# Scan mixer: in-chunk products copied out by ScalarE and added by GpSimd, VectorE's recurrence in one piece

## The reference, cut to what matters

```python
def s5_mixer(h, lam_re, ..., d_skip, w_glu):
    u = hf.reshape(b, s, S5_GROUPS, S5_GROUP)
    y_fwd = _s5_direction(u, ..., False)     # hs[t] = lam_bar * hs[t-1] + B u[t];  y = Re(C hs)
    y_bwd = _s5_direction(u, ..., True)
    y = (y_fwd + y_bwd).reshape(b, s, d) + d_skip.astype(jnp.float32) * hf
    g = jax.nn.gelu(y).astype(h.dtype)
    val, gate = jnp.split(g @ w_glu, 2, axis=-1)
    return val * jax.nn.sigmoid(gate)
```

## Time and profile before

| | us |
|---|---|
| median of 3 runs (lowest, highest) | 3253.74 (3252.61, 3254.21) |
| the profiled execution's own time | 3251.42 |
| its span, first to last instruction | 3249.6 |
| PE busy | 2966.4 (91%) |
| DVE, ACT, POOL busy | 1560.2, 1078.3, 248.3 |

### The profile page before, as it was taken

The page is one execution under the profiler, slowest core; times in us unless marked ns, Lnnn a source line. Parts: engine busy times, 40 slices in busy tenths (PEclk is TensorE's granted clock), DMA queues, the critical chain, the costliest instruction groups (busy, mean ns, idle before and its releaser), DMA issues.

```text
span 3249.6 us, 39097 instructions
## 1 busy us (share of the span) xinstructions
PE 2966.4 (91%) x15982; PEld 2394.7 (74%) x15982; DVE 1560.2 (48%) x2276; ACT 1078.3 (33%) x1651; POOL 248.3 (8%) x230
## 2 busy tenths in 40 slices
PE   6999997489999989989999699998999998898977
PEld 5787887377888877777787478887888886665745
DVE  5775663934434434534434654344544344534444
ACT  4332332143212224525435232222332233422233
POOL 2332220200000000000000300000100000100000
PEclk9999998699999989989999899999999999987868
DMA  3254547243443221122121322222122222111000
GB/s 111 87 160 153 154 140 244 102 141 110 123 130 104 91 91 59 52 85 74 70 95 68 128 80 103 91 104 78 58 98 92 103 91 87 53 40 39 14 26 27
DMA packets 109956, 305.30 MB, mean 94 GB/s; under 512 B 27616, under 2 KB 67872, under 8 KB 80464
## 3 DMA queue, kind: packets, MB, share of 16 engines
q1 hardware_dynamic: 104656, 281.31, 26.3%
q10 hardware_dynamic: 5120, 21.50, 1.8%
HBM read 265.11 MB, written 41.85 MB: 94 GB/s over the span
## 4 chain that ended last, share of the span: by engine, by line
PE 80%; DVE 8%; ACT 3%; issue 2%; POOL 2%; DMA 1%; SPq 0%; DVEq 0%; ACTq 0%; POOLq 0%
PE ps L94 79%; DVE s_ L121 2%; PE ps L99 1%; DVE H_ L121 1%; DVE htf_ L135 1%; ACT htf_ L117 0%; ACT hh_ L117 0%; ACT wh_ L117 0%; DVE ol_ L121 0%; DVE Pm_ L121 0%; DVE nmx_ L143 0%; ACT R_ L117 0%; DVE R_ L121 0%; DVE R_ L135 0%; ACT PT_ L117 0%
## 5 line engine op out<-in xcount | busy, mean ns | idle before, releaser
L94 PE MATMUL ps<-hh_,wh_ 128*128 128x512 f32 x2184 | 869.5, 398 | 22.2 <-DVE hl_ L121 11.1
L94 PE MATMUL ps<-hl_,wh_ 128*128 128x512 f32 x2184 | 854.8, 391 | 0.0
L94 PE MATMUL ps<-hh_,wl_ 128*128 128x512 f32 x2184 | 854.4, 391 | 0.0
L121 DVE TENSOR_TENSOR wl_<-raw_,wh_ 128x2048 fp32r<-128x2048 f32 x209 | 480.9, 2301 | 550.4 <-ACT wh_ L117 550.4
L117 ACT ACTIVATE wh_<-raw_ 128x2048 fp32r<-128x2048 f32 x209 | 399.0, 1909 | 358.0 <-PE ps L94 339.7
L94 PEld LDWEIGHTS ps<-hh_,wh_ 128*128 128x128 f32 x2184 | 412.9, 189 | 122.0 <-DVE hl_ L121 9.2
L94 PEld LDWEIGHTS ps<-hl_,wh_ 128*128 128x128 f32 x2184 | 413.4, 189 | 87.2 <-issue 3.7
L94 PEld LDWEIGHTS ps<-hh_,wl_ 128*128 128x128 f32 x2184 | 412.9, 189 | 87.5
L94 PE MATMUL ps<-ah_,wl_ 128*128 128x512 f32 x704 | 279.5, 397 | 0.0
L94 PE MATMUL ps<-ah_,wh_ 128*128 128x512 f32 x704 | 278.3, 395 | 0.0
L94 PE MATMUL ps<-al_,wh_ 128*128 128x512 f32 x704 | 277.7, 395 | 0.0
(11 more groups left out here) (319 smaller groups left out, 3734.7 us busy)
## 6 DMA issues: line engine op xcount, KB each, us to landing
raw_<-in_w SPq DMA_DIRECT2D x209, 1024.0 KB, 4.9
sO<-s5ce_ SPq DMA_DIRECT2D x32, 256.0 KB, 4.0
sW<-s5wt_ SPq DMA_DIRECT2D x16, 512.0 KB, 3.7
sA<-os_ SPq DMA_DIRECT2D x24, 256.0 KB, 2.1
ol_<-sA SPq DMA_DIRECT2D x24, 256.0 KB, 3.6
sT<-sK SPq DMA_DIRECT2D x32, 128.0 KB, 3.4
sB<-mk_ SPq DMA_DIRECT2D x8, 510.0 KB, 7.7
wh_<-sW ACTq DMA_DIRECT2D x3, 1024.0 KB, 4.8
```

The source lines that it names most:

```text
L94: return self.e.matmul(out, lhsT, rhs, start=start, stop=stop, skip_group_check=True)
L121: return Nothing() if self.e is None else self.e.tensor_tensor(out, a, b, op)
```

## The change

Three things change. ScalarE copies each result of `same` from PSUM to SBUF (into the yb buffers, which are free then), between its table loads. GpSimd adds that copy to U right after its multiplication, in place of VectorE. VectorE runs the recurrence of both halves to the end without any addition between (`LEAD` goes from 18 to 24); the bias additions (`mk_<-ps,mk_`, for the next layer) and the additions of `outputs` come after it.

```diff
-LEAD = 18
+LEAD = 24
@@ s5_scalar
-    for i in range(12, NT):
+    for i in range(12, 16):
         table_load(K, ac, i)
+    for un in range(4):
+        for h in range(2):
+            k = 2 * un + h
+            ac.wait_ge(*K.at("sm", un, h))
+            if k > 3:
+                ac.wait_ge(*K.at("s.ud", k - 4))
+            ac.act(Z.yb[k % 4][:, :], K.gb["sm", un, h], ACT.Copy).then_inc(*ac.up("out", "sm", un, h))
+        table_load(K, ac, 16 + un)
@@ s5_vector
-    for un in range(4):
-        for h in range(2):
-            for _ in range(6):
-                if at[0] < 64:
-                    step_both()
-            k = 2 * un + h
-            uv = Z.U[:, 8 * k:8 * k + 8, :]
-            dv.wait_ge(*K.at("s.du", k))
-            dv.wait_ge(*K.at("sm", un, h))
-            dv.tt(uv, uv, K.gb["sm", un, h].rearrange("p (g m) -> p g m", g=8), ALU.add).then_inc(*dv.up("out", "sm", un, h))
+    while at[0] < 64:
+        step_both()
+    while at[1] < 64:
+        step(1)
     bias_vector(K, dv)
     for un in range(8):
-        for _ in range(6):
-            if at[1] < 64:
-                step(1)
         uv = Z.U[:, 8 * un:8 * un + 8, :]
         dv.wait_ge(*K.at("s.used", 12 + un))
-        dv.wait_ge(*K.at("out", "sm", un // 2, un % 2))
+        dv.wait_ge(*K.at("s.ud", un))
         dv.tt(uv, uv, K.gb["ot", un].rearrange("p (g m) -> p g m", g=8), ALU.add).then_inc(*dv.up("out", "ot", un))
@@ s5_gpsimd
         po.wait_ge(*K.at("sm", k // 2, k % 2))
-        po.tt(uv, uv, ds, ALU.mult).then_inc(*po.up("s.du", k))
+        po.tt(uv, uv, ds, ALU.mult).then_inc(*po.up())
+        po.wait_ge(*K.at("out", "sm", k // 2, k % 2))
+        po.wait_ge(*po.now())
+        po.tt(uv, uv, Z.yb[k % 4][:, :].rearrange("p (g m) -> p g m", g=8), ALU.add).then_inc(*po.up("s.ud", k))
```

## The result

The changed kernel takes 3264.28 us (median of 10 runs, 3259.14 to 3266.14), against 3252.61 for ten runs of the kernel before; the ratio is 1.0038, 95% interval 1.0028 to 1.0047. It is slower by 12 us. The profiled execution took 3261.63 us, its span is 3259.8, 10.2 more than before.

What follows compares the result with a forecast made beforehand. PE, busy 91%, was taken to bound the kernel, except in the S5 mixer, where VectorE's recurrence does. VectorE's standstill of 14.4 us less 5.1 gave +9.3 on 3253.74, so 3263.0 us (range 3258 to 3267.5).

Steps and rivals of the forecast that it cites:

- Addition 0 and the way through DRAM: Behind the recurrence: addition 0 ends at 648.4, unit 0's write and reads take 7.4 us, gelu 0 begins at 655.8.
- `outputs` 4 behind gelu 0 by ScalarE's order: After the recurrence: hf copy 4 stands behind gelu 0 on ScalarE, and PE's `outputs` 4 waits for that copy.
- C, the standstill of VectorE: In the recurrence: VectorE stands still for 24 POOL instructions, 0.60 us each, 14.4 us in all.
- formula C - 5.1: Shift of gelu 0 and all behind it: VectorE's standstill less 5.1 us, forecast as +9.3 us.
- rival B: In the recurrence: each stop costs what it costs alone or more, 0.73 us; shift 12.4 us (3266.1); chance 0.15.
- C's 1.08: Rival for the recurrence: POOL's full length, 1.08 us, counts for each of 24 stops; shift 20.8 us (3274.5); chance 0.03.
- LEAD: In the recurrence: going from 18 to 24 makes 24 single, 39 paired, 24 single steps and gives back 3.5 us.
- The rest of the chain keeps its 35.9 us and all later layers move with it: From `outputs` 4 to the GLU and on: length stays 35.9 us, everything moves as one piece by +9.3 us.
- the 9.3 forecast: Whole kernel: the forecast shift of +9.3 us, added to the median of 3253.74 us before.
- ScalarE's copies cost nothing: In the recurrence: ScalarE's copies of `same` results lie in its idle time; cost and gain nothing.

Runs made afterwards that it cites:

- e1: Kernel before with only VectorE's order changed: half 1's single steps ahead of bias and `outputs` additions; 3255.11 us, ratio 1.0014.
- e2: Changed kernel with the additions of `outputs` put back between the single steps, six steps to each; 3257.57 us, ratio 1.0018.
- e4: Changed kernel with ScalarE's hf copy of a unit ahead of gelu of unit un - 4 instead of un - 3; 3260.05 us, ratio 1.0031.
- e6: Changed kernel with hf copies one unit ahead of the gelus and the first GLU weight conversion behind gelu 4; 3261.94 us, ratio 1.0034.
- e9: Changed kernel with GpSimd's sixteen multiplications and additions spread out over the paired steps, none in a row; 3261.5 us, ratio 1.0038.
- e5: Changed kernel with LEAD back at 18 instead of 24; 3264.08 us, ratio 1.0043.
- e10: The changed kernel, unaltered, run and profiled again in a later set; 3263.09 us, ratio 1.0042 to the kernel before.
- e3: Changed kernel with GpSimd's eight additions left out, so the result lacks the in-chunk product; 3256.82 us, ratio 1.0020.

## Why the prediction was right, and where its sizes were off

The forecast was 3263.0 us and 0.29% slower; measured are 3264.28 and 0.38% (0.28 to 0.47). The order of the events was right, one term of the sum was 5.3 us too small, and luck hid about half of that: with the stops as they are, the same sum gives 3268.3 us, outside the range that was given.

*Addition 0 and the way through DRAM: right.* Gelu 0 was to begin 7.4 us after addition 0; it began 7.5 after it (addition 0 ends near 653.06, gelu 0 at 660.52). e1 shows that this order alone costs 5.8 us at gelu 0, and e2 that undoing it in the changed kernel makes gelu 0 11.6 earlier.

*`outputs` 4 behind gelu 0 by ScalarE's order: right.* 4.1 us lie between the two, 4.3 before, and e4 and e6 cut the tie. The chain of before named POOL's copies for this wait; it was ScalarE's.

*C, the standstill of VectorE: mis-sized.* I put 24 stops at 0.60, 14.4 us. The changed kernel's trace has 19.7: 7.7 for the eight additions (0.96 each), 6.5 for the eight multiplications (0.81) and 5.6 for the eight copies (0.69). Two things were wrong in that term. I took the addition for as long as the multiplication, and it is 1.31 us against 1.04; and I took a discount for standing in a row, from hf copies, which e9 shows there is not (only three of the four copies from 622.97 fell upon steps at all, and the later ones of the kernel before cost up to 0.83). With 19.7 the formula C - 5.1 gives 14.6 us; gelu 0 moved by 14.4 (112.7 against 98.3). So the stops are those of rival B, alone or more; B's price of 0.73 was still too low, and C's 1.08, the whole length, too high for every stop but the one at 580.14. The sum stood for half 1 at 646.7, `outputs` 4 near 660 and the GLU's run near 696; they came at 651.35, 664.59 and 701.87.

The Trainium skill's rule ("SBUF — State Buffer", section "Who interferes with whom"), by which the later instruction is fully blocked, is borne out: each of the 24 instructions stopped VectorE once, and behind each of the sixteen additions and multiplications, in a row or alone (e9), the stopped instruction ended only after GpSimd's had. What the prediction made of the rule, the whole length as the price, is too much: VectorE lost 0.95 of 1.31 to 1.50 us and 0.72 to 0.86 of 1.04 to 1.23. Its instruction begins 0.03 to 0.42 us behind GpSimd's, so less than the whole length is left to wait, and after GpSimd's end it needs some 0.14 us less than its own usual length (0.08, 0.15 or 0.28 for 0.22, 0.29 or 0.43).

*LEAD: right in the steps, not in the time.* At half 1 e5 has 3.0 of the 3.5 us, with 0.5 us more of stops (20.2 against 19.7), and at the next norm none; the medians are too wide to tell.

*The rest of the chain keeps its 35.9 us and all later layers move with it: nearly.* From `outputs` 4 to the GLU's run it took 37.3 us in the profiled execution and 35.3 in e10, so 35.9 was right within what executions differ. The run's first part was 2.4 us shorter in the one, as it began at the higher clock, and not in the other. At the next norm the mixer is 12.7 us longer (250.4 against 237.7), and 13.5 in e10. The later layers then keep their distance up to the norm at 2725.25 (2737.64 after), but at the next one, 3100.73, it has shrunk by 2.1 us (3111.04), and by the same 2.1 in e10. Where these 2.1 us are given back was not traced. They and the mixer's 0.7 to 1.7 us (from gelu 0 to the next norm) bring the time nearer to the 9.3 forecast than C alone would have it; the prediction had neither, so that is luck.

*ScalarE's copies cost nothing: right*, 0.6 us each, all in its idle time.

The parts add up at gelu 0: additions on GpSimd 8.0 (e3), order 5.8 (e1), LEAD 3.3 (e5), less VectorE's additions, 3.9 by my estimate, are 13.2 of 14.4 us. Of the rest the traces show 0.4 in the multiplications (6.5 us of stops against 6.1 before) and 0.6 in the hf copies (5.6 against 5.0 in e1).

## What to carry to other kernels

Work taken off the busy engine is not free if its new owner stops that engine: eight 0.5 us additions became eight stops of 0.96 us on the mean, a net loss of 4.1 us (8.0 less the estimated 3.9). The largest part of the loss is another, the new place of the `outputs` additions, with 5.8. Before moving all waiting consumers behind a serial loop, ask what the first of them starts; here 2.3 us of shorter recurrence cost 5.8 us at the next stage, because the first result opens a long path through DRAM. When one tie is cut, look for the next before counting the gain: `outputs` 4 came 10.6 us sooner in e6, and gelu 7 only 2.6, no more than two executions of one kernel differ by.

## What the runs showed of the hardware that was not expected

A GpSimd addition of two full tiles is longer than a multiplication by a broadcast one of the same shape (1.31 against 1.04 us), and stops VectorE longer (0.95 against 0.72 when alone). A stop ends with the GpSimd instruction: VectorE's own ended 0.08 to 0.28 us behind it in all sixteen cases of the changed trace, so what it costs is the more the sooner VectorE's instruction begins behind GpSimd's. Behind the hf copies of that trace it ended 0.01 to 0.18 us ahead of the end that the profile gives for the copy. One kernel can run the same 363 matmuls in 82.58 or 85.00 us, with the full clock from the first matmul or at 0.74 over the first 10 us; so 2.4 us between two variants' traces need not be the variants'. Writes of 256 KB to DRAM landed 2.0 us after their issue with no weight transfer under way, and after 4.6 and 5.9 (before) and 8.8 (e6) beside weight transfers of 1 MB.
